# A two-block transformer kernel: the second block's norms applied after the products, its small stages merged, and a longer mLSTM pipeline

## The reference

```
h = h + 0.5 * (silu(n1 @ w_gate) * (n1 @ w_up)) @ w_down     # n1 = rmsnorm(h, ffn1_norm), hidden 2816
u = rmsnorm(h, mix_norm) @ w_in                              # c_q 384, c_kv 256, k_rope 64, m_x, m_v, m_o 256, gates 16, f_in 256
q  = rmsnorm(c_q, q_norm) @ w_uq;  kv = rmsnorm(c_kv, kv_norm) @ w_ukv   # 4 heads of 128 + 64 (rope)
y  = [softmax attention, chunkwise mLSTM in both directions, 2-D DFT + map]
h = h + y @ w_out
h = h + 0.5 * swiglu(rmsnorm(h, ffn2_norm))
e = rmsnorm(p @ w_proj, post_norm);  gate = sigmoid(rmsnorm(h, gate_norm) @ w_ple_gate)   # per-layer embedding (PLE)
h = h + gate * e                                             # after layer 2: rmsnorm(h, final_norm)
```

## Time and profile before

| | us |
|---|---|
| runs shown | 4045.8, 4064.4, 4070.33; median 4064.4 |
| the profiled execution, whole | 4065.52 |
| its span, first to last instruction | 4063.8 |
| PE busy in the span | 3620.0 (89%) |
| DVE, ACT, POOL busy | 1612.9, 1334.1, 601.7 |

### The profile page before, as it was taken

One profiled execution on the slowest core, in us unless ns is written; L12 is line 12 of the kernel. 1 busy time (PEld: TensorE's weight loads), 2 busy tenths in 40 slices (PEclk: granted clock), 3 DMA queues, 4 the chain that ended last, 5 costly groups with the idle time before them and its releaser, 6 DMA issues. The chain is left out here.

```text
span 4063.8 us, 42484 instructions
## 1 busy us (share of the span) xinstructions
PE 3620.0 (89%) x15392; PEld 2824.7 (70%) x15392; DVE 1612.9 (40%) x1885; ACT 1334.1 (33%) x1911; POOL 601.7 (15%) x496
## 2 busy tenths in 40 slices
PE   8778899989789997999977799987999978699996
PEld 7675588867568884888744578865888754478874
DVE  2383533346553334332335533225332335533325
ACT  3242332234732224222324332224222333432224
POOL 0040211110221101110002211113110001311104
PEclk9895899999889998999988799999999988699998
DMA  4200123322023321332200123322333210023312
GB/s 134 72 1 1 47 93 98 104 73 78 11 73 98 103 94 49 98 103 94 79 21 27 42 83 98 104 64 71 97 97 104 74 42 26 21 84 98 107 65 66
DMA packets 77169, 294.17 MB, mean 72 GB/s; under 512 B 8560, under 2 KB 11120, under 8 KB 76784
## 3 DMA queue, kind: packets, MB, share of 16 engines
q1 hardware_dynamic: 77040, 292.45, 22.4%
HBM read 290.32 MB, written 2.10 MB: 72 GB/s over the span
## 5 line engine op out<-in xcount | busy, mean ns | idle before, releaser
L176 PE MATMUL bank<-x_high,w_high 128*128 128x512 f32 x3068 | 1226.0, 400 | 230.9 <-POOL x_low L218 140.3
L147 DVE TENSOR_TENSOR w_low<-w_raw,w_high 128x1024 fp32r<-128x1024 f32 (+2 forms) x509 | 715.8, 1406 | 1281.2 <-ACT w_high L142 1271.3
L177 PE MATMUL bank<-x_low,w_high 128*128 128x512 f32 x3068 | 1211.2, 395 | 0.0
L178 PE MATMUL bank<-x_high,w_low 128*128 128x512 f32 x3068 | 1210.0, 394 | 0.0
L176 PEld LDWEIGHTS bank<-x_high,w_high 128*128 128x128 f32 x3068 | 586.3, 191 | 403.7 <-issue 178.7
L178 PEld LDWEIGHTS bank<-x_high,w_low 128*128 128x128 f32 x3068 | 586.3, 191 | 124.7
L177 PEld LDWEIGHTS bank<-x_low,w_high 128*128 128x128 f32 x3068 | 587.4, 191 | 118.7 <-issue 1.0
L142 ACT CAST w_high<-w_raw 128x1024 fp32r<-128x1024 f32 (+2 forms) x509 | 551.5, 1083 | 284.8 <-PE bank L178 279.8
L178 PE MATMUL bank<-hidden_high,w_low 128*128 128x512 f32 x1056 | 410.8, 389 | 0.0
L176 PE MATMUL bank<-hidden_high,w_high 128*128 128x512 f32 x1056 | 410.8, 389 | 0.0
L177 PE MATMUL bank<-hidden_low,w_high 128*128 128x512 f32 x1056 | 410.8, 389 | 0.0
(11 more groups left out here) (395 smaller groups left out, 3292.8 us busy)
## 6 DMA issues: line engine op xcount, KB each, us to landing
w_raw<-in_stream SPq DMA_DIRECT2D x393, 512.0 KB, 3.5
w_raw<-in_stream SPq DMA_DIRECT2D x96, 704.0 KB, 4.0
dft_positions<-in_dft SPq DMA_DIRECT2D x2, 2048.0 KB, 7.3
w_raw<-in_stream SPq DMA_DIRECT2D x4, 576.0 KB, 3.6
h<-in_x SPq DMA_DIRECT2D x8, 256.0 KB, 5.9
w_raw<-in_stream SPq DMA_DIRECT2D x16, 128.0 KB, 2.0
out<-result SPq DMA_DIRECT2D x4, 512.0 KB, 2.7
ple_p<-in_p SPq DMA_DIRECT2D x2, 512.0 KB, 3.7
```

The source lines that it names most:

```text
L147: self.nc.vector.tensor_tensor(self.lo[:, j % 2, 0:size], self.raw[:, j % RAW_SLOTS, 0:size], self.hi[:, j % 2, 0:size].bitcast(F32), ALU. ...
L176: nc.tensor.matmul(out, lhs[0], rhs[0], start=start, stop=False)
L177: nc.tensor.matmul(out, lhs[0], rhs[1], start=False, stop=False)
L178: return nc.tensor.matmul(out, lhs[1], rhs[0], start=False, stop=stop)
```

## The change

- **Split ahead of the norm.** `rms_ffn_stage`, `second_in_stage` and `ple_stage` take `x_high` and `x_low` of `h` times the gain only. The stage before makes them (`Handover`), tile by tile, right after each tile of `h` is written: ACT rounds `h * gain` and squares `h`, DVE makes the low part in one instruction. 1/rms is applied to the results: in the FFN DVE multiplies the gate product by it before Silu, and POOL multiplies Silu's result by it once more (so that the up product is scaled too). The sums over partitions are made by PE after the first job of the next stage, and ACT's Ln and Exp follow. The first FFN of each layer splits `h` itself, at its start.
- **Merged stages.** `second_in_stage` does `w_in`, the latent norms, q, k, v, the rope and, in layer 1, the rope tables, in one stage of 18 jobs. `ple_stage` does both PLE products in one stage of 16 jobs; its input p is fetched in the FFN before. `latent_norms_stage`, `rope_stage`, `rope_table_stage` and `ple_stages` are gone.
- **Evacuation moves from ACT to DVE** in these stages, and ACT and DVE split job j+2 in step j, ahead of serving job j (`lead=2`).
- **mLSTM steps.** PE accumulates three steps later, and the subtraction moves from POOL to DVE, after the next step's multiply.
- `w_out` splits its input into buffers of its own; several scratch tiles now lie in shared buffers, in the first block too.

The diff, cut to its core:

```diff
+    def next(self, part, eng, S, off, k, u, lead=1):
...
-        part(eng, S, off, k, u + 1, size)
+        part(eng, S, off, k, u + lead, size)
+    def job(self, part, eng, S, j):
+        if self.base + j < len(self.sizes):
+            part(eng, S, 0, 0, j, self.sizes[self.base + j])
...
+    def high(self, nc, C, act, S, t):
+        nc.scalar.activation(C.xhi[:, t, :], C.h[:, t, :], ACT.Identity, scale=self.gain(t)).then_inc(S.next_high, 1)
+    def square(self, nc, C, act, S, t, squares):
+        if t == DT - 1:
+            nc.scalar.activation(C.sq_last[:, :], C.h[:, t, :], ACT.Square).then_inc(S.squared, 1)
+            return
+        if t >= 2:
+            act.wait_ge(S.sq_added, max(1, t - 2))
+        nc.scalar.activation(squares[:, t % 2, :], C.h[:, t, :], ACT.Square).then_inc(S.squared, 1)
...
+    def dve_adds(self, nc, C, dve, S, k, u, h_sum):
+        t = u + 4 * k
+        dve.wait_ge(S.next_high, t + 1)
+        nc.vector.scalar_tensor_tensor(C.xlo[:, t, :], C.h[:, t, :], self.gain(t), C.xhi[:, t, :].bitcast(F32),
+                                       ALU.mult, ALU.subtract).then_inc(S.next_low, 1)
...
+def row_sums(nc, C, pe, S, bank):
+    nc.tensor.matmul(bank[:, :], C.ones_mean, C.sq_sum[:, :], start=True, stop=False)
+    nc.tensor.matmul(bank[:, :], C.ones_mean, C.sq_last[:, :], start=False, stop=True).then_inc(S.row_sums, 1)
+def rstd_chain(nc, C, act, S):
+    act.wait_ge(S.row_sums, 1)
+    nc.scalar.activation(C.rstd[:, :], C.bank[6][:, :], ACT.Ln, bias=C.eps[EPS_2]).then_inc(S.logged, 1)
+    act.wait_ge(S.logged, 1)
+    nc.scalar.activation(C.rstd[:, :], C.rstd[:, :], ACT.Exp, scale=-0.5).then_inc(S.rstd_in, 1)
...
-def latent_norms_stage(nc, C, x, groups):
...
+def rms_ffn_stage(nc, C, scale, gain=None, summed=False, after=None, p_dram=None):
...
+                    pe.wait_ge(S.hid_ready if u % 2 else S.gate_in, u // 2 + 1 + 2 * k)
+                    for q in range(DT):
+                        if gain and is_first(k, u):
+                            pe.wait_ge(S.x_low, q + 1)
+                        mm = three(nc, C.bank[u][:, :], W.parts(0, u, q * P),
+                                   (C.xhi[:, q, :], C.xlo[:, q, :]), q == 0, q == DT - 1)
+                    mm.then_inc(S.multiplied, 1)
+                    if is_first(k, u) and not summed:
+                        row_sums(nc, C, pe, S, C.bank[6])
...
+                if gain:
+                    for t in range(DT):
+                        nc.scalar.activation(C.xhi[:, t, :], C.h[:, t, :], ACT.Identity,
+                                             scale=gain(t)).then_inc(S.x_high, 1)
+                        if t == 3:
+                            W.job(W.high, act, S, 1)
...
+                    W.next(W.high, act, S, 0, k, u, 2)
+                    if is_first(k, u):
+                        rstd_chain(nc, C, act, S)
+                    if u % 2 == 0:
+                        act.wait_ge(S.gate_in, u // 2 + 3 + 2 * k)
+                        nc.scalar.activation(gated[:, u // 2, :], gated[:, u // 2, :],
+                                             ACT.Silu).then_inc(S.gate_ready, 1)
+                    else:
+                        act.wait_ge(S.hid_ready, u // 2 + 3 + 2 * k)
+                        nc.scalar.copy(hhi[:, bass.ds(u // 2 + 2 * k, 1), :],
+                                       hidden[:, u // 2, :]).then_inc(S.hid_high, 1)
...
+                    pool.wait_ge(S.gate_ready, u + 1 + 4 * k)
+                    nc.gpsimd.tensor_tensor(gated[:, u % 2, :], gated[:, u % 2, :], C.rstd[:, :],
+                                            ALU.mult).then_inc(S.gate_scaled, 1)
+                    pool.wait_ge(S.hid_high, u + 1 + 4 * k)
...
+                    W.next(W.low, dve, S, 0, k, u, 2)
+                    dve.wait_ge(S.multiplied, u + 3 + 4 * k)
+                    if u % 2 == 0:
+                        if is_first(k, u):
+                            dve.wait_ge(S.rstd_in, 1)
+                        dve.wait_ge(S.hid_ready, u // 2 + 1 + 2 * k)
+                        nc.vector.tensor_tensor(gated[:, u // 2, :], C.bank[u][:, :], C.rstd[:, :],
+                                                ALU.mult).then_inc(S.gate_in, 1)
+                    else:
+                        dve.wait_ge(S.gate_scaled, u // 2 + 1 + 2 * k)
+                        dve.wait_ge(S.hid_low, u // 2 + 1 + 2 * k)
+                        nc.vector.tensor_tensor(hidden[:, u // 2, :], C.bank[u][:, :],
+                                                gated[:, u // 2, :], ALU.mult).then_inc(S.hid_ready, 1)
...
...
+                        after.dve_adds(nc, C, dve, S, 0, t, None)
...
+def second_in_stage(nc, C, L, prj, mv, mix, qs, kn, v):
...
+                    if j == 0:
+                        row_sums(nc, C, pe, S, C.bank[6])
+                        for b in range(NB):
+                            at = slice(b * P, (b + 1) * P)
...
+                        mm.then_inc(S.row_sums, 1)
+                    if j == 8:
+                        pe.wait_ge(S.lat_summed, 3)
+                        pe.wait_ge(S.rstd_in, 2)
+                        nc.tensor.matmul(C.bank[4][:, :], C.ones, mix[:, 0, :], start=True, stop=True)
+                        nc.tensor.matmul(C.bank[5][:, :], C.ones, mix[:, 3, :], start=True, stop=True)
+                        for b in range(NB):
+                            mm = nc.tensor.matmul(C.bank[7][:, b:b + 1], mix[:, 3, b * P:(b + 1) * P],
+                                                  C.ones[:, 0:1], start=True, stop=True)
+                        mm.then_inc(S.lat_sums, 1)
...
+                for j, tiles, kt, x0 in ((uq, 3, 3, 0), (uq + 1, 3, 3, 0), (kn_job, 4, 2, 3)):
+                    pe.wait_ge(S.low_ready, j + 1)
+                    pe.wait_ge(S.lat_low, x0 + kt)
+                    for t in range(tiles):
+                        pe.wait_ge(S.evacuated, n_of[j] + t + 1)
+                        for q in range(kt):
+                            mm = three(nc, C.bank[(n_of[j] + t) % 4][:, :], W.parts(0, j, (t * kt + q) * P),
+                                       (lat_hi[:, x0 + q, :], lat_lo[:, x0 + q, :]), q == 0, q == kt - 1)
+                        if t < tiles - 1:
+                            mm.then_inc(S.tiled, 1)
+                    mm.then_inc(S.multiplied, 1)
+                    if j == uq:
+                        pe.wait_ge(S.k_copied, 2)
+                        pe.wait_ge(S.evacuated_tok, NB)
+                        turn(2, C.bank[4])
+                pe.wait_ge(S.evacuated, 4 + 18)
+                turn(0, C.bank[6])
+                turn(1, C.bank[7])
+                pe.wait_ge(S.low_ready, v_job + 1)
+                for b in range(NB):
+                    if b == 0 or b >= 2:
+                        pe.wait_ge(S.sin_done, max(b, 1))
+                    for q in range(2):
+                        xs = (lat_hi[:, 3 + q, b * P:(b + 1) * P], lat_lo[:, 3 + q, b * P:(b + 1) * P])
+                        mm = three(nc, C.bank[4 + b][:, :], xs, W.parts(0, v_job, q * T, T), q == 0, q == 1)
+                mm.then_inc(S.multiplied, 1)
...
+                    if j == uq + 1:
+                        sines(2, 0, C.bank[4])
+                    if j in n_of:
...
+                        for t in range(tiles):
...
+                            nc.vector.tensor_tensor(dst[t], C.bank[(n + t) % 4][:, :], r,
+                                                    ALU.mult).then_inc(S.evacuated, 1)
+                        if j == uq + 1:
+                            dve.wait_ge(S.evacuated, 4 + 18)
+                            cosines(0)
+                            cosines(1)
+                        if j == kn_job:
+                            sines(0, 1, C.bank[6])
+                            sines(1, 2, C.bank[7])
...
-def rope_table_stage(nc, C):
...
-def rope_stage(nc, C, qr, prj, kr):
...
-                    if s >= 2:
-                        accumulate(s - 2)
+                    if s >= 3:
+                        accumulate(s - 3)
+                accumulate(N - 3)
...
-            @block.gpsimd
-            def _(pool):
-                for m in range(N):
+                def low(m):
+                    dve.wait_ge(S.high_ready, m + 1)
+                    nc.vector.tensor_tensor(w_lo[:, m % 4, lo:hi], wf[:, m % 4, lo:hi],
...
+                    if s:
+                        low(s - 1)
+                    if s >= U and s % U in (1, 2):
+                        numerators_out(2 * (h - 1) + s % U - 1)
...
+def ple_stage(nc, C, L, last):
...
+                for j in range(jobs):
+                    pe.wait_ge(S.low_ready, j + 1)
+                    pe.wait_ge(S.evacuated, j + 1)
+                    kt, xhi, xlo = (2, p_hi, p_lo) if j < DT else (DT, C.xhi, C.xlo)
+                    for q in range(kt):
+                        if j == 0:
+                            pe.wait_ge(S.p_low, q + 1)
```

(60 more changed lines are left out.)

657 lines of the change are left out of this document (450 added, 207 removed).

## The result

The changed kernel takes 3924.7 us (median of 4 runs, 3922.3 to 3926.8) against 4064.9 us: a ratio of 0.968, 95% interval 0.965 to 0.971. Its profiled execution took 3926.8 us with a span of 3925.1, 138.7 less than the span before.

A forecast was written before the change was run, and what follows sets the result against it. The prediction took PE, busy 89% of the span, as the bound, with gains at stage boundaries and in mLSTM steps. Its terms summed to 145.3 us, which from 4065.5 gave 3920; the range was 3870 to 3985.

The forecast's parts named there:

- Layer norm to FFN1: Boundary before each layer's first FFN, counted once: second job earlier by 17.9 us, less 2 for a slow clock: 16.
- w_out to FFN2: Boundary before the second FFN, twice: 19.6 us becomes 10.7, less 1.7 for the clock: 7.2 each, 14.4.
- PLE to the next FFN: Boundary after the PLE, once: 21.7 us becomes 16.4, gain 5.3, less 1.7 for the clock: 3.6.
- FFN to w_in: Boundary before the input projection, twice: 19.8 us becomes 12.4, less 1.7 for the clock: 5.7 each, 11.4.
- Rival (2): Waits of 3.1 us no longer lower the clock, mLSTM runs at full level: 26 us more gain, 3894; chance 0.10.
- Projections to attention: Merged projection stage, twice: gain 22.4 us despite two stalls, less 1.7 for the clock, plus 3: 23.7 each, 47.4.
- 3 back: Projections window and opening of attention: fewer waits mean less time at the slow clock, 3 us regained per layer.
- PLE: PLE products, twice: 18.0 us less 1.5 for the clock, plus 2.5 in the gate jobs: 19 each, 38.
- Rival (1): Merged stages choke on written order, results served behind splits, DVE carrying ACT's evacuations: 3975 us; chance 0.18.
- mLSTM: 32 steps, twice: 8 of the idle 17.3 us saved per layer, 16 in all; bounds nothing to 15 per layer.
- The end: End of the kernel: the longer finish of the PLE stage costs 1.5 us.
- Why the FFN stays as it is: FFN jobs: chains of 5.0 us fit inside PE's 5.42 per job, so PE's rate stays; no gain or loss counted.

The follow-up runs named there:

- in_step: Changed kernel with rstd_columns 512 bytes wide per partition instead of 32, so every buffer behind it starts 480 bytes later: 3900.8 us, ratio 0.964 to the kernel before.
- order: Changed kernel, rstd_columns 128 bytes wide; in the merged projection stage VectorE serves q and k results before splitting weights, rope of k after: 3926.8 us, 0.968.
- warm: Changed kernel, rstd_columns 128 bytes wide; TensorE issues products nobody reads during its waits at the second block's boundaries: 3907.7 us, 0.964.
- combined: in_step plus the edits of warm and order, and TensorE instead of GpSimd summing the PLE's squares of e: 3864.2 us, 0.954.

## Why the prediction was right

The time was 4.7 us above the forecast, and the range held it. The mechanism was right at the boundaries; that the total came so close is in part luck, for two items of 16 and 21 us that no term had nearly cancel.

- **Layer norm to FFN1, w_out to FFN2, PLE to the next FFN: right.** By the windows 18.2 for 16, 7.5 for 7.2 twice, 4.2 for 3.6. With buffers in step the whole pieces agree within about 2 us.
- **FFN to w_in: mechanism right, the clock's term too small.** The wait was 3.43 in layer 1 and 3.85 in layer 2 (said: 3.1) and the column sums 1.8. "About 1.7 us of it" for the slow clock was 3.0 in layer 1 and 1.5 in layer 2. The gains are 4.6 and some 5.6 for 5.7 each. Rival (2), that such a wait leaves the clock alone, came true at one boundary of 32, in in_step.
- **Projections to attention: the stage right, the "3 back" wrong.** Up to the first score the gain is 20.5 in layer 1 and 18.9 in layer 2, for 22.4 - 1.7 = 20.7. The window is 48.0; the latent sums cost 2.6 in place of 3.1. Both stalls are there as read from the code (2.98 and 0.9). The failed step is "with fewer waits I expect 3 back", behind the first score. From there to the first mLSTM step layer 1 lost 2.4 (105.9 us for 103.5) and layer 2 won 1.0 (103.2 for 104.1). The ten profiles with the changed stages have 99.4 to 106.1 there, 103.2 on the mean, and the four with the old ones 103.1 to 104.7, 103.6 on the mean: no 3 came back. The stall's own slow products also cost more than the 1.7 charged: order won 7.0 by taking away 3.9 of idle time.
- **PLE: right, by its own steps.** Small jobs 2.89 us apart (3.0), second gate job after 36.6 (36.2), the gate jobs behind it 38.7 for 41.4 (2.7 gained, 2.5 said). Only the wait ahead of the first small job was longer, 4.66 for 3.1. Rival (1) was wrong here.
- **mLSTM: 13.2 a layer for 8, a term of the right sign and the wrong size.** "DVE subtracts in 0.69 or less ... and one more step is in flight" named two halves and priced neither. Put in alone, the third step brings 12.5 and the engine 4.6; together they bring 13.2. The 8 were taken out of idle time. The windows show idle time of 12.3 for 17.3, and busy time of 45.1 for 53.3 for the same 168 products, with the granted clock at 0.71 for 0.65: most of the gain is faster products, which only the upper bound of 15 had named.
- **The end: 3.9 lost for 1.5** (7.8 us from the last gate product to the last matmul, for 3.8). The last square sum waits for GpSimd, whose add started at 3906.32 and took 1.77 us beside a finish of VectorE, and the row sums run at the slow level. Timeline of the changed kernel:

```profile
3906.27 0.69 DVE L2647 TENSOR_TENSOR h<-h,ple_gate 128x512 f32<-128x512 f32 x1
3906.32 1.77 POOL L386 TENSOR_TENSOR sq_sum_and_last<-sq_sum_and_last,squares 128x512 f32<-128x512 f32 x1 [2.82 <-ACT squares L377]
3908.15 2.08 PE L2565 MATMUL bank<-sq_sum_and_last,consts 128*128 128x512 f32 x2 [4.68 <-POOL sq_sum_and_last L386]
```

- **"Why the FFN stays as it is": half wrong.** The up phase does stay, with nearly twice GpSimd's busy time (12.65 and 23.73 us in 100). The down phase lost 3.5 us six times, 21 us that no term had, through 32 bytes. The text had named it ("wrong if that FFN count falls") without a price. With the distance put right, in in_step, the second block gains 147.8 for the 145.3 predicted.
- **The first block's clock gave some 16 us.** Corrected for its two down phases, 1537.1, in the profile of before, was the longest of 14, and the changed kernel's 1521.3 the fifth longest. The prediction started from one profiled execution, 1.1 us above the median of three, and had no means to see that. This and the 21 us nearly cancel, which is luck. Either of them alone would have left the time inside the range.

## What to carry to other kernels

Keep what TensorE streams a multiple of 512 bytes a partition away from its weights (here 32, 64 and 128 past one were slower), for instance by giving every buffer between them such a size, and after any new allocation count the matmuls in 100 us of a steady stretch of code that was not touched. For a chain over several engines, ask first how many steps are in flight and only then which engine does which part: here an operation nearly twice as long cost 0.7 us in 32 steps once a third step was there to cover it. In a kernel that is bound by TensorE, compare pieces between events that both traces have, for an unchanged part can differ by more than the change that is being measured.

## What the runs showed of the hardware

- Products of a 128x128 weight tile with 512 fp32r columns start 0.2267 us apart when the moving operand's distance from w_high is a multiple of 512 bytes a partition (in all 14 profiles for x_high and x_low, in 7 for hidden), 0.2333 at 32 and 128 past one, 0.2289 at 64 (hidden), with the granted clock at 1.00 in each. 256 was not run.
- The same idle time of 3.43 us cost the job behind it 2.9 to 3.0 us in five of eight profiles, 1.8 in two and nothing to speak of (0.1) in one; idle times of 1.1 to 1.6 us, at eight boundaries of warm and combined, cost nothing.
- A split of 256 columns on VectorE took 1.30 us beside a GpSimd add and 0.43 without.
